# Recurrence of a two-block network: scores of the step beyond ahead of the output products, behind one product nobody reads

## What is computed

```python
num = inter_w[..., None] * jnp.einsum('bhtd,bhde->bhte', qc, c_mat) + jnp.einsum('bhts,bhsd->bhtd', s, vc)
den = inter_w * jnp.einsum('bhtd,bhd->bht', qc, n_vec) + jnp.sum(s, axis=-1)
h = num / jnp.maximum(jnp.abs(den), jnp.exp(-m_t))[..., None]
...
c_new = carry_w[..., None, None] * c_mat + jnp.einsum('bhs,bhsd,bhse->bhde', w, kc, vc)
n_new = carry_w[..., None] * n_vec + jnp.einsum('bhs,bhsd->bhd', w, kc)
```

## Time and profile before

| | |
|---|---|
| median of 3 runs | 3457.02 us (3452.78 to 3458.35) |
| the profiled execution, its own time | 3456.51 us |
| its span in the trace | 3454.3 us |
| TensorE busy | 3236.7 us, 94% of the span |
| VectorE, ScalarE, GpSimd busy | 1582.2, 1220.2, 79.3 us |
| mean granted clock of TensorE | 0.952 of full |
| first product of the recurrence | 1875.13 us after the start of the span |
| first product of the stage behind it | 1983.10 us |

### The profile page before, as it was taken

How to read it: one execution, slowest core, us unless ns; L and a number is a source line. 1 busy time by engine, 2 the same in 40 slices (tenths; PEclk the granted TensorE clock), 3 DMA queues, 4 the chain that set the end, 5 groups by cost and what they waited for, 6 DMA issues and landing times. The chain is left out here.

```text
span 3454.3 us, 39285 instructions
## 1 busy us (share of the span) xinstructions
PE 3236.7 (94%) x15176; PEld 2524.5 (73%) x15176; DVE 1582.2 (46%) x2389; ACT 1220.2 (35%) x2022; POOL 79.3 (2%) x84
## 2 busy tenths in 40 slices
PE   7898999999999899998997798899999987989999
PEld 6586677773477677775885686788888865768887
DVE  3754466661154466665424543333333424344444
ACT  2344233332464333335213353422222334543332
POOL 4100000000000000000001100000000000000000
PEclk9959999999998999998999898899999989999999
DMA  4201343431311243440111000112111110012221
GB/s 160 74 1 49 122 170 146 170 125 19 55 49 49 98 158 128 164 158 19 62 49 49 1 1 25 49 49 73 49 73 63 59 49 25 1 58 90 95 97 73
DMA packets 160791, 259.35 MB, mean 75 GB/s; under 512 B 58476, under 2 KB 73194, under 8 KB 160556
## 3 DMA queue, kind: packets, MB, share of 16 engines
q1 hardware_dynamic: 158932, 252.94, 20.7%
q10 hardware_dynamic: 1628, 4.76, 0.3%
q0 software_dynamic: 128, 0.26, 0.0%
HBM read 255.85 MB, written 2.10 MB: 75 GB/s over the span
## 5 line engine op out<-in xcount | busy, mean ns | idle before, releaser
L1171 ACT ACTIVATE w_hi<-wbuf 128x1024 fp32r<-128x1024 f32 x330 | 348.5, 1058 | 1247.9 <-PE psA L750 1198.7
L748 PE MATMUL psA<-act_hi,w_hi 128*128 128x512 f32 (+1 forms) x1824 | 702.0, 385 | 61.8 <-DVE act_lo L1782 41.5
L749 PE MATMUL psA<-act_lo,w_hi 128*128 128x512 f32 (+1 forms) x1824 | 686.3, 376 | 0.0
L750 PE MATMUL psA<-act_hi,w_lo 128*128 128x512 f32 (+1 forms) x1824 | 685.6, 376 | 0.0
L1776 DVE TENSOR_TENSOR w_lo<-wbuf,w_hi 128x1024 fp32r<-128x1024 f32 x330 | 404.1, 1227 | 560.9 <-ACT w_hi L1171 556.7
L748 PE MATMUL psA<-hid_hi,w_hi 128*128 128x512 f32 (+1 forms) x1280 | 476.8, 372 | 3.2
L749 PE MATMUL psA<-hid_lo,w_hi 128*128 128x512 f32 (+1 forms) x1280 | 472.0, 369 | 0.0
L750 PE MATMUL psA<-hid_hi,w_lo 128*128 128x512 f32 (+1 forms) x1280 | 471.3, 368 | 0.0
L748 PEld LDWEIGHTS psA<-act_hi,w_hi 128*128 128x128 f32 x1824 | 350.9, 192 | 148.1 <-issue 52.4
L749 PEld LDWEIGHTS psA<-act_lo,w_hi 128*128 128x128 f32 x1824 | 352.1, 193 | 60.5 <-issue 3.6
L750 PEld LDWEIGHTS psA<-act_hi,w_lo 128*128 128x128 f32 x1824 | 350.9, 192 | 61.9
(11 more groups left out here) (230 smaller groups left out, 3594.5 us busy)
## 6 DMA issues: line engine op xcount, KB each, us to landing
wbuf<-in_mlp_w_dram SPq DMA_DIRECT2D x64, 2048.0 KB, 7.8
work<-in_ada_w_dram SPq DMA_DIRECT2D x32, 1536.0 KB, 10.9
wbuf<-in_ab_w_in_dram SPq DMA_DIRECT2D x10, 1024.0 KB, 5.0
wbuf<-in_ple_w_gate_dram SPq DMA_DIRECT2D x4, 2048.0 KB, 7.5
wbuf<-in_hy_w_in_dram SPq DMA_DIRECT2D x3, 2048.0 KB, 7.8
wbuf<-in_c_w_in_dram SPq DMA_DIRECT2D x3, 2048.0 KB, 7.5
wbuf<-in_hy_w_out_dram SPq DMA_DIRECT2D x2, 2048.0 KB, 8.0
wbuf<-in_mla_w_out_dram SPq DMA_DIRECT2D x2, 2048.0 KB, 7.8
```

Of the source, the lines that this page charges most:

```text
L748: pe.matmul(psA[:, s, a:b], w_hi, x_hi[:, a:b], start=first, stop=False)
L749: pe.matmul(psA[:, s, a:b], w_hi, x_lo[:, a:b], start=False, stop=False)
L750: ins = pe.matmul(psA[:, s, a:b], w_lo, x_hi[:, a:b], start=False, stop=last)
L1171: return nc.scalar.activation(out, in_, func, **kw)
```

## The change

Two things change on TensorE alone. Within the loop `lstm_scores(u + 2)` is called ahead of `lstm_values(u)` and no longer behind it. And each `lstm_scores`, the two ahead of the loop too, begins with one `keep_clock` product into columns 0 to 511 of its own slot, behind the wait for the slot and ahead of the `pick` products. The L1107 products overwrite what it leaves.

```diff
@@ -1099,6 +1099,7 @@
 
                 s, c = A("lstm", u)
                 pe.wait_ge(a_free[s], c)
+                keep_clock(psA[:, s, 0:512], 1)
                 cols = slice(t * P, t * P + P)
                 for h in range(A_H):
                     pe.matmul(psA[:, s, 512 + h * P:512 + h * P + P], C["pick"][0:4, h * P:h * P + P],
@@ -1134,9 +1135,9 @@
             lstm_keys(*lstm_steps[0])
             for step in lstm_steps:
                 u = step[0]
-                lstm_values(*step)
                 if u + 2 < len(lstm_steps):
                     lstm_scores(*lstm_steps[u + 2])
+                lstm_values(*step)
                 if u + 1 < LSTM_KV:
                     lstm_keys(*lstm_steps[u + 1])
             keep_clock(psA[:, 0, 0:512], 8)
```

## The result

| | before | changed |
|---|---|---|
| median | 3454.93 us (4 runs, 3452.78 to 3458.35) | 3432.57 us (4 runs, 3430.41 to 3435.62) |
| ratio | | 0.9937, 95% interval 0.9925 to 0.9949 |
| span of the profiled execution | 3454.3 us | 3431.6 us |

The changed kernel is 22.4 us faster. The forecast was 3441 us with a range from 3435 to 3449, so the direction was right and the gain was more than the range allowed. In the two traces the stage, from its first product to the first product behind it, went from 107.97 us (1875.13 to 1983.10) to 86.89 (1874.44 to 1961.33): 21.1 of the 22.7 us lie there. The other 1.6 lie in code that is the same in both, 0.7 ahead of the stage and 0.9 behind it.

A forecast was written before the change was run, and what follows sets the result against it. The recurrence's ring of waits between TensorE and VectorE was taken as the bound. Terms 16.5 + 4.4 + 0.8 - 6.0 = 15.7 us gained gave 3441 us, range 3435 to 3449.

The forecast's parts named there:

- eight steps 46.4 for 62.9 us: Middle of the recurrence, values of step 1 to step 9: 5.8 us a step, 16.5 us gained.
- prologue: Stage start: two unread products at half clock delay the first values; 6.0 us lost, bounds 2.7 to 9.1.
- values 9 to 10, 5.1 for 9.5: Step after the eight: no scores between its values any more, one ring of 5.1 us, 4.4 gained.
- tail behind that: Values 10 to 11, last values and eight unread products: clock expected to fall, 0.8 us gained.
- The ring: Recurrence: values, scores, mask and finish chain TensorE and VectorE, 7.3 us; new order shortens it to 5.1, TensorE bounds at 5.8.
- The waits as cause of the falls: Recurrence: each fall to half clock follows a TensorE wait of more than 2 us; without waits, full clock.
- (d): Rival, recurrence: clock stays at half through the stage, 36 us lost, 3493 us; 6%.
- (c): Rival, recurrence: clock falls as often as before for another reason, three slow steps take back 15.9 us, 3457; 8%.
- (b): Rival, recurrence: VectorE's drains and waits for ScalarE hold steps at about 6.6 us, 6.4 less gained, 3447.5; 10%.
- The sign set for it: Prologue: the forecast is right if values of step 0 start at 1891 to 1894.
- a bound that "needs everything on one side": Whole kernel: gain bounded by 9.4 and 23 us, both ends judged unlikely; 11 to 21 kept.
- the starting point: Whole kernel: gain subtracted from the profiled execution's 3456.5 us, with 0.5 added for the median of the runs.

The follow-up runs named there:

- g2: The changed kernel run a third time, nothing altered: 2 us or so apart from its first run, 3434.87 us, 0.9944 of the kernel before.
- f4: The changed kernel run a second time, nothing altered, on another chip than its third run: 3437.97 us, 0.9949 of the kernel before.
- e1: The changed kernel without its unread products, so the new order of scores and values alone: 3427.00 us, 0.9920 of the kernel before.
- e4: The changed kernel with two unread products a step instead of one: 3442.97 us, 0.9965 of the kernel before.
- e2: The kernel before, old order kept, with one unread product added ahead of every scores piece: 3469.11 us, 1.0037 of the kernel before.
- f1: The new order alone, plus three unread products ahead of the meeting before the stage: 3431.24 us, 0.9930 of the kernel before.
- e3: The changed kernel with unread products only from step 2 on, none in the prologue: 3433.11 us, 0.9935 of the kernel before.
- f2: The new order alone, plus unread products in the tail's waits, three before values of step 10, two before step 11: 3429.99 us, 0.9926 of before.
- g3: The new order alone, without unread products, repeated beside the changed kernel: 3427.66 us, 0.9922 of the kernel before.

## Why the prediction was wrong in size

By its own steps, with the stages of the traces:

| step of the forecast | forecast | first trace, g2 | f4 |
|---|---|---|---|
| eight steps 46.4 for 62.9 us | 16.5 | 17.2 | 17.2 |
| prologue | -6.0 | -3.7 | -6.0 |
| values 9 to 10, 5.1 for 9.5 | 4.4 | 4.5 | 4.5 |
| tail behind that | 0.8 | 3.1 | 1.4 |
| sum | 15.7 | 21.1 | 17.1 |

- **The ring, right.** The order takes the scores out of the ring, TensorE becomes the bound, the round was put at 5.8 and is 5.71. e1 and e4 show the two engines on either side of it: 5.4 us where VectorE is the bound, 6.57 where TensorE has one more product. That 5.8 came so near is partly rounding: the pieces named (1.96, 1.08, 1.0, 0.97 and 0.86) add up to 5.87, which would have given 47.0 us for eight steps and 15.9 gained. From start to start the values then took 1.79 us and not 1.96 (1895.59 to 1897.38), as there is no wait ahead of them, and the keys 0.89 and not 0.97; the product took 0.95.
- **The waits as cause of the falls, right for the middle.** All steps of the middle are at 1.00 in every kernel with the new order, with or without products. The clock fell there in both traces of before, and oftener in e2, where the wait stayed. But a wait of over 2 us is not what it takes: in f1 the clock fell some 2 us behind one of 0.99 us, while one of 1.08 us in the prologue of the changed kernel (1885.66 to 1886.74) had no fall behind it. Whether the length of a wait counts, or the idle share around it, these runs do not separate. One reading under (d) is wrong: the clock did not rise again in each slow step, since it was at half from the step 9 to 10 on into the unread products. Rivals (c) and (d) are out. Rival (b), VectorE's delays, is out too: 5.4 us is its round.
- **The prologue, mis-sized.** "I take 6.0 lost, between the first two, since nothing fixes when the clock rises." It was 3.7 in two traces of three and 6.0 in one. That lies between the bounds of 2.7, for a rise ahead of scores(1), and 4.7, for one behind the keys: the clock rose at 1882.90, as the `pick` products of step 1 ran. The sign set for it, values(0) at 1891 to 1894, came at 1889.88. The step that failed is where the term let the clock rise, behind the keys or later; in two traces it rose during the scores of step 1. Whether the unread products brought that about is open (e3). The rule of the Trainium skill (TensorE: Matmul & The Clock Gate, What's actually happening), by which activity brings the clock up, was nearer to the 3.7 than the 6.0 that I set against it. It is not sufficient: f4 lost just 6.0, with 15.25 us at half clock in which TensorE was busy for 14.99.
- **The tail, mis-sized.** "The waits of 2.4 to 3.1 us are still there, so I expect the clock to fall, and take 0.6 gained, between nothing and 1.8." In the first trace it fell only behind the start of the last values, so that values 10 to 11 took 4.40 us for 6.16 before (1.8 gained, not 0.6), and the last values with the eight products 10.63 us for 12.00 (1.4 gained, not 0.2). In f4 it fell a step earlier, and the first of these was nothing.
- **The range, too narrow below.** Both terms were set near their slow ends, and a gain of up to 23 us stood in the text as a bound that "needs everything on one side". Two of three traces came near it. Over its 16 runs the changed kernel lies between 3429.3 and 3443.4 us, with a median of 3435.3, 20 us below the kernel before. The four runs behind the 3432.57 were on its fast side, which the range should have allowed for. And some 2 of the 8.4 us between forecast and result lie in the starting point: the forecast subtracts from 3457.02 us, the median of three runs, which with a fourth is 3454.93 and in the later groups 3454.6 to 3455.7.

What decides between a prologue of 21.15 and one of 23.42 us is open. The instructions are the same, and in both the clock's last fall lies some 5 us ahead of the stage's first product (within 1869 to 1870 for a first product at 1874.44, within 1870 to 1871 for one at 1875.85). The views show no difference ahead of the rise. f4 ran on another chip than g2, but the spread is there on one chip too: the six runs of g2 lie between 3429.3 and 3440.5 us.

## What to carry to other kernels

Look for the ring: if two engines both have idle time, each ended by the other, and neither is full, follow one round and ask for each piece whether its place in the program or its data put it there. Here the scores could be multiplied a step ahead, and moving them in the code took 28 us (e1). Products that only keep TensorE busy cost their whole time where it is the bound or where they lie in the ring (e4, e2); here the change would have been 6 to 7 us better without its own. Where TensorE waits anyway they may give something: the trace of f2 has 1.7 us in the tail, though the whole time does not show it.

## What the runs showed of the hardware

- TensorE can be busy for 15 us at half clock (f4, 14.99 of 15.25 us), while in another execution of the same instructions the clock is up after 8.5 us.
- The clock fell shortly behind waits of 2.1 to 2.4 us in a ring with TensorE busy for 5.09 of 7.28 us, and at the same three steps in two executions of before; a change of 0.86 us in the ring (e2) made it fall in more of them. In the prologue of f1 it fell some 2 us behind a wait of 0.99 us.
- Outside the stage the same code took 3341.7 us in one trace (span less stage, e1) and 3348.5 in another (e3). A single whole time thus tells a gain of 5 us poorly, while the stage alone repeats to 0.1 us in e1 and g3 (83.15 and 83.13) and in before (107.97 and 108.09), though not in f4.
